# SSD scan of a hybrid layer: token columns and decay rows made once, the first tile in the last projection step, tiled matmul groups adjacent

## The chip, the cores and the metric

The kernel runs on one core of one Trainium2 chip. The metric is the device time of one execution in microseconds (us). Five engines work beside each other on the core: TensorE (PE; its weight loads have rows of their own, PEld), VectorE (DVE), ScalarE (ACT), GpSimd (POOL) and SyncE (SP), which only issues transfers.

## The reference

One layer of a streaming encoder for 1024 prompt tokens and 64 new tokens of another sequence (1088 tokens, width 1024, f32): FFN1, a token mixer of three head groups (SSD, GLA, forgetting attention), FFN2. The change concerns the SSD scan, 8 heads of 64, 2 groups of B and C, state 128. Cut to that:

```python
acum = jnp.cumsum(dt * A, axis=2)                       # within a chunk
cb = jnp.einsum('bclgn,bcsgn->bclsg', Cm, Bm)[..., hg]
seg = acum[:, :, :, None, :] - acum[:, :, None, :, :]
decay = jnp.where(causal, jnp.exp(jnp.where(causal, seg, 0.0)), 0.0)
y_intra = jnp.einsum('bclsh,bcsh,bcshp->bclhp', cb * decay, dt, x)
decay_end = jnp.exp(acum[:, :, -1:, :] - acum)
states = jnp.einsum('bclh,bclhn,bclhp->bchpn', decay_end * dt, Bh, x)
h = h * exp(acum[:, -1]) + states                        # scan over chunks, h0 first
y_inter = jnp.einsum('bclhn,bchpn,bclh->bclhp', Ch, h_prev, jnp.exp(acum))
y = y_intra + y_inter + ssd_d * xs                       # then * silu(z), norm, w_out
```

The prompt starts from a zero state, the 64 new tokens from a given one.

## The kernel before

All work lies on one core, and the order of every engine is written out by hand, with semaphores between engines. The layer runs FFN1, then 13 projection steps (`IN_PLAN`, t = 0 to 12, `proj_pe`, matmuls in the helper `three`, L169), then the SSD stage, the output projection (`out_pe`) and FFN2. Each projection step has up to two column blocks of three pieces of some 363 tokens; ACT reads each piece out of PSUM (L1328 copies, L1332 the Silu of the gates). Between the steps stand the small stages: the attention before t = 4, the GLA gate before t = 5, the GLA scan before t = 7 (`gla_pe`, `gla_act`, `gla_dve`), the convolution of x, B and C beside t = 7 to 10 (`conv_pool`, `conv_act`). t = 11 and 12 make the gates z. Small rows needed by the SSD scan (dt in `small`, the cumulated dt*A in `adt`) come out of step 2; `ssd_prep_dve` makes the cumulated sums by a scan. Eight of these rows, one for each head, hold all 1088 tokens. POOL sends `adt` to `a_kept` in HBM, and SP loads it back as a broadcast over 128 partitions, tile by tile, into `ab` (L2852, 512 KB each).

The SSD stage has nine tiles j, eight of 128 tokens and one of 64, the chunks of the scan. Its order on PE (`ssd_pe`): front(j) transposes B (L2066), the two small rows (L2067 and L2068, 8x128 each) and x (L2070) to token-major; cb(j) makes the scores of C and B (L2078); back(j) makes y and the state: H·cea, eight heads as 64-column matmuls (L2105), D times x (L2111), the tile's state (L2116), then x·dt times the masked scores, again eight heads in 64 columns (L2123). L2089 makes the sums for the norm of y, for two tiles at once. In the loop front(j+1) comes before back(j) and cb(j+1) after it.

ACT (`ssd_act`) makes exp of the decay rows of every tile (`ea`, L2165), copies B out of PSUM (L2171), two small exps (L2172, L2174), eight relus of a_s − a_l (L2180) and their exp (L2184); then squares, Ln and Exp for the norm, and casts of the mixed tiles for the output projection (L2191). The projection's Silu and these Exp are in different activation tables (loads at L1907, L2143 and at the first Silu). DVE (`ssd_dve`) copies the small columns (L2255, L2258), multiplies x by dt (`xdt`, L2285) and by dt times the decay to the end (`xde`, L2289), masks the scores (L2295), multiplies them into the decay (L2299), and updates the state: ht = H times the tile's decay (L2266), H = ht + state (L2271), and z = z times y (L2276). The decay in L2266 is read out of PSUM. POOL (`ssd_pool`) makes `dx` (D on the diagonal, L2334), `cea` = C times `ea` (L2320, two ops for a tile), the norm's multiplication (L2330) and the low parts of the mixed tiles (L2345). Behind the loop ACT and DVE split z for the output projection (`ssd_hi`, `ssd_lo`, L2224).

In the GLA stage ACT loads a table (L1907) and copies the outputs (L1910); DVE masks scores (L1988), takes the state out of PSUM (L1997) and updates S, with S and the new state in SBUF (L2012); PE's L1850 reads S. POOL has nothing to do there.

Of the kernel before, what the change touches and what calls it, by code (L numbers as in the profile page):

```python
# [2047 lines left out]

def ssd_pe(K, e, M):
    nc = K.nc  # L2050
    g = slice(SMALL_DT, SMALL_DT + SSD_H)
# [1 line left out]
    e.wait_ge(M.acum, 1)
    e.wait_ge(M.xc, 16)
    e.wait_ge(M.H, 1)

    def front(j):

        a, r = TILES[j]
        bank = 2 + j % 2  # L2060
        wait(e, M.b_read, j - 1)
        wait(e, M.sm_read, j - 1)
        wait(e, M.x_read, j - 1)
        wait(e, M.hupd, j - 1)
        for u in range(2):
            nc.tensor.transpose(K.ps[:r, bank, P * u:P * u + P], K.xc[:, 4 + u, a:a + r], K.ident)  # L2066
        nc.tensor.transpose(K.ps[:r, bank, 256:264], K.adt[g, a:a + r], K.ident[g, g])  # L2067
        nc.tensor.transpose(K.ps[:r, bank, 264:272], K.small[g, a:a + r], K.ident[g, g]).then_inc(M.b_mm, 1)  # L2068
        for u in range(4):
            mm = nc.tensor.transpose(K.ps[:r, j % 2, P * u:P * u + P], K.xc[:, u, a:a + r], K.ident)  # L2070
        mm.then_inc(M.x_mm, 1)

    def cb(j):

        a, r = TILES[j]
        wait(e, M.m, j)
        for u in range(2):
            mm = nc.tensor.matmul(K.ps[:r, 4, P * u:P * u + r], K.xc[:, 4 + u, a:a + r],  # L2078
                                  K.xc[:, 6 + u, a:a + r], start=True, stop=True)
        mm.then_inc(M.cb2_mm, 1)  # L2080
# [1120 lines left out]
```

## Time and profile before

| what | value |
|---|---|
| median of three runs | 2030.64 us (2027.94 to 2032.79) |
| the profiled execution, its own time | 2030.71 us |
| its span in the profile | 2028.9 us |
| granted TensorE clock | 0.998 |
| PE busy | 1990.9 us, 98% of the span |
| last projection matmul ends | 1158.67 us |
| SSD stage, to the first matmul of the output projection | 1158.67 to 1218.03 us |

The span is the time between the first and the last instruction that the profiler records; the execution's time has some 1.8 us around it. Times of rows are us from the span's start. An engine's idle time costs something only where PE waits for it. The start of a weight load (PEld) is a good mark for when a matmul group begins, as PE's own ends are modelled.

### The profile page before, as it was taken

To read this page: it belongs to the slowest core of one execution; us is meant where nothing else is said; L and a number is where in the kernel's file an instruction comes from. 1 tells how busy PE (TensorE), PEld (TensorE's weight loads), DVE (VectorE), ACT (ScalarE), POOL (GpSimd) and SP (SyncE) were. 2 spreads that over 40 slices of the span, in tenths; PEclk is the share of its full clock that TensorE was granted. 3 is DMA by queue.
4 is the path that set the end of the run, shared out by engine and by line. 5 is a ranking of instruction groups with operands and counts; after the bars stand their busy time and mean duration, and the time that the engine had idled before them with its cause. 6 is when DMAs were issued, how large, how long until landed. Compare 5 with 4: busy or idle time off the path is not lost.

```text
span 2028.9 us, 36007 instructions
## 1 busy us (share of the span) xinstructions
PE 1990.9 (98%) x15223; PEld 1935.0 (95%) x15223; DVE 1196.0 (59%) x1658; ACT 780.6 (38%) x1268; POOL 235.6 (12%) x295
## 2 busy tenths in 40 slices
PE   7999999999999999999999999999999999999999
PEld 7899999999999989768899989999999999999999
DVE  5955655556776752555555183377555565577674
ACT  6433333334333352664242393244333333343331
POOL 0000000000000340251011072100000000000000
PEclk9999999999999999999999999999999999999999
DMA  4222232225976514211011123312322223378654
GB/s 153 81 86 102 86 126 85 86 102 189 364 282 230 199 50 183 99 34 43 23 44 43 53 84 140 123 55 86 125 85 87 102 92 123 116 304 329 254 217 160
DMA packets 67330, 265.04 MB, mean 131 GB/s; under 512 B 7709, under 2 KB 20621, under 8 KB 57825
## 3 DMA queue, kind: packets, MB, share of 16 engines
q1 hardware_dynamic: 51648, 198.89, 27.2%
q0 software_dynamic: 15520, 63.83, 8.1%
q8 instruction: 121, 1.98, 0.4%
q14 instruction: 41, 0.33, 0.1%
HBM read 203.52 MB, written 59.18 MB: 129 GB/s over the span
## 4 chain that ended last, share of the span: by engine, by line
PE 90%; DVE 4%; DMA 3%; ACT 2%; issue 1%; POOL 0%; SPq 0%; DVEq 0%; ACTq 0%; POOLq 0%
PE ps L169 82%; PE ps L1485 1%; DMA h_kept<-sb_hs_b_last 1%; PE ps L1529 1%; PE ps L1511 1%; DMA sb_h_raw<-h_kept 1%; PE ps L247 1%; DVE sb_x L509 0%; DVE sb_xl L563 0%; PE ps L2123 0%; PE ps L2111 0%; PE ps L2089 0%; DVE sb_xl L499 0%; DMA sb_x<-x 0%; DMA sb_down_raw<-wb 0%
## 5 line engine op out<-in xcount | busy, mean ns | idle before, releaser
L169 PE MATMUL ps<-sb_xh,sb_up_hi 128*128 128x272 f32 x2400 | 692.0, 288 | 6.4 <-DVE sb_x L2448 2.0
L169 PE MATMUL ps<-sb_xl,sb_up_hi 128*128 128x272 f32 x2400 | 692.2, 288 | 0.0
L169 PE MATMUL ps<-sb_xh,sb_up_lo 128*128 128x272 f32 x2400 | 690.0, 287 | 0.0
L169 PEld LDWEIGHTS ps<-sb_xh,sb_up_hi 128*128 128x128 f32 x2400 | 452.9, 189 | 7.8 <-DVE sb_up_lo L454 2.3
L169 PEld LDWEIGHTS ps<-sb_xh,sb_up_lo 128*128 128x128 f32 x2400 | 452.4, 189 | 0.0
L169 PEld LDWEIGHTS ps<-sb_xl,sb_up_hi 128*128 128x128 f32 x2400 | 452.2, 188 | 0.1
L169 PE MATMUL ps<-sb_h_hi,sb_down_hi 128*128 128x272 f32 x1188 | 342.5, 288 | 0.6 <-DVE sb_down_lo L1049 0.4
L169 PE MATMUL ps<-sb_h_hi,sb_down_lo 128*128 128x272 f32 x1188 | 342.9, 289 | 0.0
L169 PE MATMUL ps<-sb_h_lo,sb_down_hi 128*128 128x272 f32 x1188 | 341.9, 288 | 0.0
L169 PE MATMUL ps<-sb_nh,sb_whi 128*128 128x362 f32 (+1 forms) x696 | 231.0, 332 | 2.4 <-DVE sb_nl L376 1.5
L169 PE MATMUL ps<-sb_nl,sb_whi 128*128 128x362 f32 (+1 forms) x696 | 228.3, 328 | 0.0
L169 PE MATMUL ps<-sb_nh,sb_wlo 128*128 128x362 f32 (+1 forms) x696 | 228.2, 328 | 0.0
L169 PEld LDWEIGHTS ps<-sb_h_hi,sb_down_hi 128*128 128x128 f32 x1188 | 223.5, 188 | 1.0 <-DVE sb_down_lo L1049 1.0
L169 PEld LDWEIGHTS ps<-sb_h_lo,sb_down_hi 128*128 128x128 f32 x1188 | 223.8, 188 | 0.0
L169 PEld LDWEIGHTS ps<-sb_h_hi,sb_down_lo 128*128 128x128 f32 x1188 | 223.4, 188 | 0.0
L447 ACT CAST sb_up_hi<-sb_up_sum 128x512 fp32r<-128x512 f32 x160 | 99.5, 622 | 241.2 <-PE ps L169 222.8
L454 DVE TENSOR_TENSOR sb_up_lo<-sb_up_raw,sb_up_hi 128x512 fp32r<-128x512 f32 x132 | 90.7, 691 | 132.9 <-ACT sb_up_hi L447 132.9
L1043 ACT CAST sb_down_hi<-sb_down_raw 128x1408 fp32r<-128x1408 f32 x54 | 74.2, 1374 | 225.2 <-PE ps L169 215.0
L169 PEld LDWEIGHTS ps<-sb_nh,sb_whi 128*128 128x128 f32 x696 | 130.7, 188 | 5.9 <-issue 2.3
L1162 DVE SCALAR_TENSOR_TENSOR sb_x<-ps,sb_x 128x544 f32<-128x544 f32 x96 | 65.4, 720 | 114.8 <-PE ps L169 114.8
L169 PEld LDWEIGHTS ps<-sb_nl,sb_whi 128*128 128x128 f32 x696 | 130.7, 188 | 0.6
L169 PEld LDWEIGHTS ps<-sb_nh,sb_wlo 128*128 128x128 f32 x696 | 130.7, 188 | 0.0
(340 smaller groups left out, 2729.1 us busy)
## 6 DMA issues: line engine op xcount, KB each, us to landing
sb_down_raw<-wb SPq DMA_DIRECT2D x92, 704.0 KB, 5.4
sb_up_raw<-wa SPq DMA_DIRECT2D x44, 1024.0 KB, 4.8
sb_h_raw<-h_kept SPq DMA_DIRECT2D x60, 544.0 KB, 6.0
sb_wraw<-wm SPq DMA_DIRECT2D x17, 1024.0 KB, 4.8
h_kept<-sb_hs_b POOLq DMA_DIRECT2D x20, 816.0 KB, 4.7
...
```

The source lines that it names most:

```text
L169: mm = K.nc.tensor.matmul(out, a, b, start=first and n == 0, stop=last and n == 2, skip_group_check=loose)
L247: mm = K.nc.tensor.matmul(K.ps[:, bank, :Q], K.ones, first_squares(K, c)[:, k], start=k == 0, stop=k == KT - 1)
L447: K.nc.scalar.copy(up_slot(K, n)[0], up_weight(K, n)).then_inc(N.f.ahi, 1)
L454: K.nc.vector.tensor_tensor(lo, up_weight(K, n), hi.bitcast(F32), ALU.subtract).then_inc(N.f.alo, 1)
L1043: K.nc.scalar.copy(down_slot(K, g)[0][:], down_raw(K, g, 0)).then_inc(N.f.bhi, 1)
L1162: K.nc.vector.scalar_tensor_tensor(out=x, in0=bank2(K, 2 * (g % 4)), scalar=0.5 * sign, in1=x, op0=ALU.mult, op1=ALU.add).then_inc(N.f.x_u ...
L1485: mm = nc.tensor.matmul(K.psf[:r, at:at + n], K.fq[o, m, a:a + r], rhs[o], start=True, stop=True)
L1511: mm = nc.tensor.transpose(K.ps[:w, 4 + n % 3, i * P:i * P + r], K.pr[u % PR][:r, k:k + w], K.ident[:r, :r])
L1529: mm = nc.tensor.matmul(K.ps[64 * s:64 * s + 64, 7, :r], v, K.pt[:w, s, i, :r], start=i == 0, stop=i == len(tiles) - 1)
```

## The change

1. **Token columns.** `ssd_tok_pe`, before projection step 8, transposes three rows of eight heads for all nine tiles (27 transposes of 8 rows): `adt`, dt, and dt times the decay to the end of the chunk. `ssd_tok_act` copies them to `tok` with two copies. The two small transposes, three small DVE operations and two small exps of each tile go.
2. **Decay rows.** `ssd_prep_dve` also makes a(end) − a (two subtractions). In the GLA stage ACT takes exp of both rows (8x1088 each) between the table load and the first copy; POOL sends exp(a) to `ea_kept` in HBM and multiplies the other by dt. SP loads `ea` of tiles 2 to 8 as a broadcast, as it does `ab`; tile 1's is still an exp on ACT. The state's decay, in L2266 before read out of PSUM, is now read from `ea` in SBUF.
3. **First tile.** After piece 3 of the last projection step PE does transposes and scores of tile 0 (banks 7, 6 and 4); ACT does its copy and relus after reading piece 2 and its exp after piece 3; DVE follows. Its operands have buffers of their own.
4. **Zero state.** Tile 0 has no H·cea matmuls and no `cea`; the first H is a copy of its state out of PSUM, and the memset goes.
5. **Order in back(j).** D times x, then the state, then H·cea and x·dt times scores, both in 64 columns, next to each other. The state's matmul thus comes before H·cea, and waits for xde and for the last H.
6. `dx` is made by POOL at the end of the convolution.

The core of the diff:

```diff
+        if t == IN_STEPS - 1 and n == IN_START[t] + FIRST_TILE_AT:
+            e.wait_ge(M.xc, 16)
+            ssd_front_pe(K, e, M, 0)
+            ssd_cb_pe(K, e, M, 0)
...
+    g = slice(SMALL_DT, SMALL_DT + SSD_H)
+    e.wait_ge(M.acum, 1)
+    nc.scalar.activation(K.ge[g, :], K.adt[g, :], ACT.Exp).then_inc(M.gexp, 1)
+    e.wait_ge(M.gqk, 1)
+    nc.scalar.activation(K.ga[g, :], K.go[g, 1], ACT.Exp).then_inc(M.gexp, 1)
+    e.wait_ge(M.gexp, 6)
...
+def ssd_rows_pool(K, e, M, ea_kept):
+    g = slice(SMALL_DT, SMALL_DT + SSD_H)
+    e.wait_ge(M.gexp, 5)
+    e.dma_start(ea_kept, K.ge[g, :]).then_inc(M.a_out, 16)
+    e.wait_ge(M.gexp, 6)
+    K.nc.gpsimd.tensor_tensor(K.ga[g, :], K.ga[g, :], K.small[g, :], ALU.mult).then_inc(M.pad, 1)
...
+def ssd_tok_pe(K, e, M):
+
+    g = slice(SMALL_DT, SMALL_DT + SSD_H)
+    e.wait_ge(M.st_read, GCH)
+    e.wait_ge(M.pad, 2)
+    for j, (a, r) in enumerate(TILES):
+        for q, rows in enumerate((K.adt, K.small, K.ga)):
+            at = 3 * SSD_H * j + SSD_H * q
+            mm = K.nc.tensor.transpose(K.ps[:r, 7, at:at + SSD_H], rows[g, a:a + r], K.ident[g, g])
+    mm.then_inc(M.b_mm, 1)
+
+
...
     def back(j):
 
         a, r = TILES[j]
+        xdt, xde, btok, seg = ssd_operands(K, j)
         wait(e, M.y2, j)
-        wait(e, M.hst_read, j)
-        if j == NTT - 1:
-            e.wait_ge(M.H, 2)
         y = K.ps[:, 5].rearrange("p (t q) -> p t q", t=4)
-        for h in range(SSD_H):
-            o = 64 * (h % 2)
-            if h % 4 == 0:
-                e.wait_ge(M.cea, 2 * j + h // 4 + 1)
-            mm = nc.tensor.matmul(y[o:o + 64, h // 2, :r], K.H[:, 64 * h:64 * h + 64], K.cea[:, j % 2, h, :r],
-                             start=h < 2, stop=False, skip_group_check=True)
-        mm.then_inc(M.h_read, 1)
         if j == 0:
             e.wait_ge(M.dx, 1)
         for u in range(4):
-            nc.tensor.matmul(y[:, u, :r], K.dx[:, u], K.xc[:, u, a:a + r], start=False, stop=False,
+            nc.tensor.matmul(y[:, u, :r], K.dx[:, u], K.xc[:, u, a:a + r], start=u == 0, stop=False,
                              skip_group_check=True)
-        e.wait_ge(M.b_read, j + 1)
+        e.wait_ge(M.b_read, j + 2)
         e.wait_ge(M.x_read, j + 1)
+        wait(e, M.hst_read, j)
         for u in range(2):
-            mm = nc.tensor.matmul(K.ps[:, 6, 256 * u:256 * u + 256], K.btok[j % 2][:r, P * u:P * u + P],
-                                  K.xde[:r, 256 * u:256 * u + 256], start=True, stop=True)
+            mm = nc.tensor.matmul(K.ps[:, 6, 256 * u:256 * u + 256], btok[:r, P * u:P * u + P],
+                                  xde[:r, 256 * u:256 * u + 256], start=True, stop=True)
         mm.then_inc(M.hst_mm, 1)
+        if j == NTT - 1:
+            e.wait_ge(M.H, 1)
+        if j:
+            for h in range(SSD_H):
+                o = 64 * (h % 2)
+                if h % 4 == 0:
+                    e.wait_ge(M.cea, 2 * (j - 1) + h // 4 + 1)
+                mm = nc.tensor.matmul(y[o:o + 64, h // 2, :r], K.H[:, 64 * h:64 * h + 64], K.cea[:, j % 2, h, :r],
+                                      start=False, stop=False, skip_group_check=True)
+            mm.then_inc(M.h_read, 1)
         e.wait_ge(M.m, j + 1)
         e.wait_ge(M.xdt, j + 1)
         for h in range(SSD_H):
             o = 64 * (h % 2)
-            mm = nc.tensor.matmul(y[o:o + 64, h // 2, :r], K.xdt[:r, 64 * h:64 * h + 64], K.seg[:r, j % 2, h, :r],
+            mm = nc.tensor.matmul(y[o:o + 64, h // 2, :r], xdt[:r, 64 * h:64 * h + 64], seg[:r, h, :r],
                                   start=False, stop=h >= 6, skip_group_check=True)
         mm.then_inc(M.y_mm, 1)
 
...
+    ssd_front_pe(K, e, M, 1)
+    ssd_cb_pe(K, e, M, 1)
     for j in range(NTT):
-        if j + 1 < NTT:
-            front(j + 1)
+        if 0 < j < NTT - 1:
+            ssd_front_pe(K, e, M, j + 1)
         back(j)
-        if j + 1 < NTT:
...
+def ssd_tok_act(K, e, M):
+
+    def copy():
+        e.wait_ge(M.out, 16 * (3 + 2 * GLA_H))
+        e.wait_ge(M.b_mm, 1)
+        tiles = K.ps[:, 7, :NTT * 3 * SSD_H].rearrange("p (j n) -> p j n", j=NTT)
+        K.nc.scalar.copy(K.tok[:, :NTT - 1], tiles[:, :NTT - 1])
+        K.nc.scalar.copy(K.tok[:TS, NTT - 1], tiles[:TS, NTT - 1]).then_inc(M.b_read, 1)
+
+    return {-1: copy}
+
...
+def ssd_first_act(K, e, M):
+
+    def tokens():
+        ssd_btok_act(K, e, M, 0)
+        ssd_seg_act(K, e, M, 0)
+
+    return {FIRST_TILE_AT - 1: tokens, FIRST_TILE_AT: lambda: ssd_exp_act(K, e, M, 0)}
 
...
+    M.dve(V.tensor_tensor_scan(K.adt[g, :], K.go[g, 1], K.go[g, 0], 0.0, ALU.mult, ALU.add))
+    for a, b, n in ((0, TP, P), (TP, T, TS)):
+        rows = K.adt[g, a:b].rearrange("p (c l) -> p c l", l=n)
+        to_end = V.tensor_tensor(K.go[g, 1, a:b].rearrange("p (c l) -> p c l", l=n),
+                                 rows[:, :, n - 1:n].to_broadcast([SSD_H, (b - a) // n, n]), rows, ALU.subtract)
+    to_end.then_inc(M.acum, 1)
...
+    def state(j):
+
         a, r = TILES[j]
...
+        if j == 0:
+            e.wait_ge(M.hst_mm, 1)
+            V.tensor_copy(K.H[:], K.ps[:, 6]).then_inc(M.hst_read, 1)
+        else:
+            e.wait_ge(M.h_read, j)
+            dst = K.Hp if j == TP // P - 1 else K.H
+            V.tensor_tensor(K.ht[:].rearrange("p (h q) -> p h q", h=SSD_H), hv,
+                            K.ea[:, j % 2, :, r - 1:r].to_broadcast([P, SSD_H, SSD_P]), ALU.mult).then_inc(M.hupd, 1)
+            e.wait_ge(M.hupd, j)
+            e.wait_ge(M.hst_mm, j + 1)
+            V.tensor_tensor(dst[:], K.ht[:], K.ps[:, 6], ALU.add).then_inc(M.hst_read, 1)
         if j == TP // P - 1:
             e.wait_ge(M.cache, 16 * (5 + GLA_H))
...
+        px = K.ps[:r, tile_banks(j)[0]].rearrange("p (h q) -> p h q", h=SSD_H)
+        for dst, at, done in ((xdt, SSD_H, M.xdt), (xde, 2 * SSD_H, M.x_read)):
+            V.tensor_tensor(heads(dst, r), px, K.tok[:r, j, at:at + SSD_H].rearrange("p (h o) -> p h o", o=1)
+                            .to_broadcast([r, SSD_H, SSD_P]), ALU.mult).then_inc(done, 1)
...
+    tokens(0)
+    decayed(0)
+    tokens(1)
+    state(0)
+    decayed(1)
+    for j in range(2, NTT):
+        state(j - 1)
+        tokens(j)
+        decayed(j)
...
+        if j == 1:
+            e.wait_ge(M.ea, 1)
+        else:
+            e.wait_ge(M.ea_in[j % 2], 16 * ((j - j % 2) // 2))
+        wait(e, M.h_read, j - 2)
...
+                    sp.wait_ge(M.a_out, 32)
                     sp.wait_ge(K.w_lo, 2 * s)
                     for j, (a, r) in enumerate(TILES):
-                        if j > 1:
-                            sp.wait_ge(M.ea, j - 1)
-                            sp.wait_ge(M.seg, j - 1)
+                        wait(sp, M.seg, j - 1)
+                        if j == 3:
+                            sp.wait_ge(M.ea, 1)
                         sp.dma_start(K.ab[:, j % 2, :, :r], o["a_kept"][:, a:a + r].partition_broadcast(P))\
                             .then_inc(M.a_in[j % 2], 16)
-                    sp.wait_ge(M.ea, NTT)
+                        if j < 2:
+                            continue
+                        if j == 2:
+                            sp.wait_ge(M.proj_mm, IN_START[IN_STEPS])
+                        else:
+                            sp.wait_ge(M.cea, 2 * (j - 2))
+                            sp.wait_ge(M.hupd, j - 2)
+                        sp.dma_start(K.ea[:, j % 2, :, :r], o["ea_kept"][:, a:a + r].partition_broadcast(P))\
+                            .then_inc(M.ea_in[j % 2], 16)
```

`ssd_front_pe` and `ssd_cb_pe` are front(j) and cb(j) as functions, without the small transposes.

## Rows read from the trace of the kernel before

**Rows 1.** the page, part 1: engine, busy us, share of the span, instructions.

```profile
PE 1990.9 (98%) x15223; PEld 1935.0 (95%) x15223; DVE 1196.0 (59%) x1658; ACT 780.6 (38%) x1268; POOL 235.6 (12%) x295
```

**Rows 2.** chain of waits, window 1157 to 1225: start us, us, engine, tile, line.

```profile
1159.18 1.28 ACT L2143
...
1160.48 1.06 ACT sb_ea L2165
...
1161.98 2.37 ACT sb_seg L2180 x8
...
1165.54 1.30 DVE sb_seg L2299 x2
```

**Rows 3.** windows: us; busy of PE, PEld, DVE, ACT, POOL; granted clock; DMA share; GB/s.

```profile
1166.88:1172.54 5.66, 5.66 (x56) 4.58 (x56) 5.52 (x12) 5.45 (x16) 3.00 (x3) 1.00 0.42 125
...
1183.88:1191.28 7.40, 7.40 (x66) 6.06 (x65) 5.40 (x12) 7.34 (x17) 4.98 (x3) 1.00 0.25 74
...
1209.92:1215.80 5.88, 5.88 (x57) 4.80 (x56) 5.27 (x11) 4.84 (x13) 2.59 (x3) 1.00 0.48 163
```

**Rows 4.** timeline of PE's weight loads, one tile: start, us, line, operands.

```profile
1173.57 0.52 PEld L2078 LDWEIGHTS ps<-sb_xc 128*128 128x128 f32 x4 [0.17 <-issue]
1174.01 0.25 PEld L2066 LDWEIGHTS ps<-sb_const,sb_xc 128*128 128x128 f32 x2
1174.43 0.13 PEld L2067 LDWEIGHTS ps<-sb_const,sb_cum 8*128 8x128 f32 x1 [0.17 <-issue]
1174.48 0.14 PEld L2068 LDWEIGHTS ps<-sb_const,sb_small 8*128 8x128 f32 x1
1174.64 0.42 PEld L2070 LDWEIGHTS ps<-sb_const,sb_xc 128*128 128x128 f32 x4
...
1176.26 0.97 PEld L2111 LDWEIGHTS ps<-sb_xc,sb_dx 128*128 128x128 f32 x8 [0.17 <-issue]
1177.14 0.73 PEld L2116 LDWEIGHTS ps<-sb_xde,sb_btok 128*128 128x128 f32 x4
1178.21 0.85 PEld L2123 LDWEIGHTS ps<-sb_seg,sb_xdt 128*64 128x64 f32 x16 [0.33 <-issue]
```

**Rows 5.** timeline of ACT, the last gate piece; in brackets the idle time before.

```profile
1158.69 0.47 ACT L1332 ACTIVATE sb_z<-ps 128x362 f32<-128x362 f32 x1 [3.53 <-PE ps L169]
```

**Rows 6.** timeline of DVE, the same tile.

```profile
1173.69 0.69 DVE L2276 TENSOR_TENSOR sb_z<-sb_z,ps 128x512 f32<-128x512 f32 x1 [0.28 <-PE ps L2123]
1174.29 0.68 DVE L2285 TENSOR_TENSOR sb_xdt<-ps,sb_tk 128x512 f32<-128x512 f32 x1
```

**Rows 7.** timeline of POOL in the SSD stage.

```profile
1177.91 2.51 POOL L2320 TENSOR_TENSOR sb_cea<-sb_xc,sb_ea 128x512 f32<-128x512 f32 x2 [3.33 <-ACT sb_ea L2165]
1180.38 2.52 POOL L2345 TENSOR_TENSOR sb_nl<-sb_fq,sb_nh 128x1088 fp32r<-128x1088 f32 x1
...
1219.97 2.37 POOL L2330 TENSOR_TENSOR sb_z<-sb_z,sb_scratch 128x1024 f32<-128x1024 f32 x1 [2.43 <-ACT sb_scratch L2159]
```

**Rows 8.** the tile ht: ns min/median/max, first and last start.

```profile
L2266 DVE TENSOR_TENSOR sb_ht<-sb_H,ps x9: 673/680/683, 1166.7 to 1214.6; 128x512 f32<-128x512 f32 x9
```

**Rows 9.** DMA of line L2852 (decay rows): us from issue to landing.

```profile
DMA to landing us min/median/max: 3.8/3.8/5.7
```

**Rows 10.** timeline of DVE behind the SSD loop.

```profile
1217.31 2.12 DVE L2224 SCALAR_TENSOR_TENSOR sb_nl<-sb_z,sb_vec,sb_nh 128x364 fp32r<-128x364 f32 x4 [0.31 <-ACT sb_nh L2215]
1220.71 2.02 DVE L2224 SCALAR_TENSOR_TENSOR sb_nl<-sb_z,sb_vec,sb_nh 128x362 fp32r<-128x362 f32 x1 [1.28 <-ACT sb_nh L2215]
```

**Rows 11.** line L1104 (FFN), ns min/median/max.

```profile
L1104 DVE TENSOR_TENSOR sb_h_lo<-sb_h_raw,sb_h_hi x72: 717/1285/2059, 514.0 to 1987.3; 128x1088 fp32r<-128x1088 f32 x60, 128x544 fp32r<-128x544 f32 x12
```

**Rows 12.** line L194 (norms), ns min/median/max.

```profile
L194 POOL TENSOR_TENSOR sb_rms<-sb_rms,sb_sqs x36: 817/972/2210, 680.2 to 1313.8; 128x362 f32<-128x362 f32 x24, 128x364 f32<-128x364 f32 x12
```

**Rows 13.** timeline of ACT in the GLA stage.

```profile
992.41 0.37 ACT L1910 COPY sb_go<-ps 128x256 f32<-128x256 f32 x1 [2.67 <-PE ps L1856]
```

**Rows 14.** timeline of DVE in the GLA stage.

```profile
992.25 0.48 DVE L2012 SCALAR_TENSOR_TENSOR sb_S<-sb_S,sb_glast,sb_gd 128x256 f32<-128x256 f32 x1
```

More of the change, by code:

```diff
@@ new lines, in ssd_front_pe @@
+def ssd_front_pe(K, e, M, j):
+    a, r = TILES[j]
+    x_bank, b_bank = tile_banks(j)
+    if j == 0:
+        e.wait_ge(M.b_read, 1)
+    elif j > 1:
+        e.wait_ge(M.b_read, j)
+        e.wait_ge(M.x_read, j - 1)
+    for u in range(2):
+        mm = K.nc.tensor.transpose(K.ps[:r, b_bank, P * u:P * u + P], K.xc[:, 4 + u, a:a + r], K.ident)
+    mm.then_inc(M.b_mm, 1)
+    for u in range(4):
+        mm = K.nc.tensor.transpose(K.ps[:r, x_bank, P * u:P * u + P], K.xc[:, u, a:a + r], K.ident)
+    mm.then_inc(M.x_mm, 1)
@@ L2049, in ssd_pe, with ssd_cb_pe, ssd_operands @@
+def ssd_cb_pe(K, e, M, j):
+    a, r = TILES[j]
+    wait(e, M.m, j)
+    for u in range(2):
+        mm = K.nc.tensor.matmul(K.ps[:r, 4, P * u:P * u + r], K.xc[:, 4 + u, a:a + r],
+                                K.xc[:, 6 + u, a:a + r], start=True, stop=True)
+    mm.then_inc(M.cb2_mm, 1)
+def ssd_operands(K, j):
+    if j == 0:
+        return K.xdt_first, K.xde_first, K.btok_first, K.seg_first
+    return K.xdt, K.xde, K.btok[j % 2], K.seg[:, j % 2]
 def ssd_pe(K, e, M):
     nc = K.nc
-    g = slice(SMALL_DT, SMALL_DT + SSD_H)
@@ L2052, in ssd_pe @@
     e.wait_ge(M.proj_read, IN_START[IN_STEPS])
[L2053 to L2080, printed above, removed]
     def sums(c):
@@ L2138, in ssd_pe, with ssd_btok_act, ssd_seg_act, ssd_exp_act @@
     return lambda: sums(NYP - 1)
+def ssd_tok_act(K, e, M):
+    def copy():
+        e.wait_ge(M.out, 16 * (3 + 2 * GLA_H))
+        e.wait_ge(M.b_mm, 1)
+        tiles = K.ps[:, 7, :NTT * 3 * SSD_H].rearrange("p (j n) -> p j n", j=NTT)
+        K.nc.scalar.copy(K.tok[:, :NTT - 1], tiles[:, :NTT - 1])
+        K.nc.scalar.copy(K.tok[:TS, NTT - 1], tiles[:TS, NTT - 1]).then_inc(M.b_read, 1)
+    return {-1: copy}
+def ssd_btok_act(K, e, M, j):
+    r = TILES[j][1]
+    e.wait_ge(M.b_mm, j + 2)
+    wait(e, M.hst_mm, j - 1)
+    K.nc.scalar.copy(ssd_operands(K, j)[2][:r, :], K.ps[:r, tile_banks(j)[1], 0:256]).then_inc(M.b_read, 1)
+def ssd_seg_act(K, e, M, j):
+    r = TILES[j][1]
+    seg = ssd_operands(K, j)[3]
+    e.wait_ge(M.a_in[j % 2], 16 * (j // 2 + 1))
+    wait(e, M.y_mm, j - 1)
+    for h in range(SSD_H):
+        ins = K.nc.scalar.activation(seg[:r, h, :r], K.ab[:r, j % 2, h, :r], ACT.Relu,
+                                     bias=K.tok[:r, j, h:h + 1], scale=-1.0)
+    ins.then_inc(M.seg, 1)
+def ssd_exp_act(K, e, M, j):
+    r = TILES[j][1]
+    seg = ssd_operands(K, j)[3]
+    e.wait_ge(M.seg, j + 1)
+    K.nc.scalar.activation(seg[:r, :, :r], seg[:r, :, :r], ACT.Exp, scale=-1.0).then_inc(M.eseg, 1)
+def ssd_first_act(K, e, M):
[3 more added lines that the diff above has]
+    return {FIRST_TILE_AT - 1: tokens, FIRST_TILE_AT: lambda: ssd_exp_act(K, e, M, 0)}
 def ssd_act(K, e, M):
@@ L2302, in operands, with ssd_dx_pool @@
         ins.then_inc(M.m, 1)
-    decays(0)
-    for j in range(NTT):
-        if j:
-            state(j - 1)
-        operands(j)
-    state(NTT - 1)
+    tokens(0)
[7 more added lines that the diff above has]
+        decayed(j)
+    state(NTT - 1)
+def ssd_dx_pool(K, e, M):
+    e.wait_ge(M.b_mm, 1)
+    e.wait_ge(M.a_out, 32)
+    for u in range(4):
+        ins = K.nc.gpsimd.tensor_scalar(K.dx[:, u], K.ident, K.vec[:, V_D + u:V_D + u + 1], 1.0, ALU.mult, ALU.mult)
+    ins.then_inc(M.dx, 1)
 def ssd_pool(K, e, M, outs):
@@ L2658, in __init__ @@
         self.ea = sem(tag + "ea")
-        self.de0 = sem(tag + "de0")
-        self.de1 = sem(tag + "de1")
-        self.sm_read = sem(tag + "sm_read")
+        self.ea_in = [sem(tag + f"ea_in{s}") for s in range(2)]
         self.cea = sem(tag + "cea")
```

121 lines of the change are left out of this document (46 added, 75 removed).

## The prediction

> **What bounds the kernel now.** First the page: TensorE (PE) is busy 98% of the span [rows 1]. So time is won only where PE waits or where PE's own work shrinks, and work on another engine is free until PE waits for it. Then the chain of waits through the SSD stage: after the last projection matmul at 1158.67 the chain leaves PE for ACT (table load 1.28, exp of the decay rows 1.06, eight relus 2.37, one more exp) and DVE (1.30), and PE has it back at 1166.88 [rows 2]. The table of windows, cut where the matmul group L2123 of each tile starts, shows the rest: PE is busy for the whole of every window after 1166.88, with DVE at 5.5 and ACT at 5.4 of 5.66 [rows 3]. A tile takes 5.66, one with the norm's sums 7.40. So the stage has two prices: a start of 8.2 in which PE waits for ACT and DVE, and a loop in which PE is the bound and the others are close behind. Last, PE's weight loads show the parts of one tile and the gaps between them [rows 4]. The granted clock is 1.00 (2.4 GHz) in all windows [rows 3], so no clock effect enters.
>
> E is the end of the last projection matmul, 1158.67; numbers without a unit are us.
>
> **The change part by part.**
>
> *Start (gain).* Before, L2123 of tile 1 starts at 1172.54 [rows 3], E+13.87. After, tile 0's transposes, scores and mask lie in the last projection step, so PE starts when the last gate piece is read: .02+.47+.06 = .55 [rows 5]. Then by the rows of one tile [rows 4]: transposes of tile 1 .66 (L2066 .25, L2070 .42, without the small pair), scores .44 (L2078 to L2066), tile 0's D-skip .88 (L2111 to L2116), state and gap 1.07 (L2116 to L2123), its group .85: E+4.44. Then PE to DVE .30 (idle .28 before L2276) and z .69 [rows 6], in which the transposes of tile 2 fit: D-skip of tile 1 from E+5.5, state and gap, and now H·cea .85 before the group: L2123's successor in tile 1 starts at E+8.3. The other engines are just in time [rows 2]: table load done E+1.79, exp 1.06, copy (.44 with the two small ops that go), relu 2.37, exp 1.06 at E+6.7, DVE 1.30: E+8.1. POOL's cea(1), 2.51 [rows 7] behind the first exp, is there at E+5.4. Gain 13.87 − 8.3 = **5.6**.
>
> *Loop (gain).* From tile 1 to tile 8 L2123 goes from 1172.54 to 1215.80, 43.3 [rows 3]. PE's work of a tile after: .66+.44+.88+1.07, two groups of .85, one gap of .17 = 4.91 [rows 4], against 5.66. But PE will not be the bound. The new order closes a ring: z → xdt → xde (.60+.60+.69, by the spacing of DVE's rows) → state and gap 1.07 → H·cea .85 → .30 → ht .68 → H .69 → z: 5.5 [rows 4, 6, 8]. Four steps of 5.5 and three with sums, which PE bounds (4.91 + 1.74 (7.40 − 5.66) − .17 for a gap = 6.5), make 41.5; the shorter last tile gives back .4: 41.1. Gain **2.1**. ACT loses its row exp and is no bound. SP's queue now holds two broadcasts a tile, and a load is queued behind a wait for cea and ht; one lands in 3.8, at worst 5.7 [rows 9], and ea(j) is wanted about a tile (5.5) after its issue; what is late there, 0 to .2, lies under the next term.
>
> *ht reads SBUF twice (loss).* Before, every large DVE op of the loop has one input in PSUM, and ht is .67 to .68 in all nine tiles though POOL works beside it [rows 8]. After, ht multiplies H by ea, both in SBUF. What such an op does beside POOL shows at L2224: .53 each in a row of four, but 2.02 when asked at 1220.71 [rows 10], while POOL's norm runs 1219.97 to 1222.34 [rows 7]: it ended .39 after the norm, so it got going about .2 before the norm's end. L1104, two SBUF inputs too, grows from 1.29 to 2.06 [rows 11], and POOL's L194 from .97 to 2.21 [rows 12]: each of the two loses in turn. After the change cea(j+2) starts behind H·cea and its load, some 3.95 after ht, and ht is asked again 4.8 after, inside the first half of cea (1.25) [rows 7]. So a wait of .2 to .8 a tile, and none in the tiles with sums, where PE is later anyway. I take **1.0** in all; bounds .3 (POOL elsewhere) and 2.5 (most tiles).
>
> The Trainium skill ("SBUF — State Buffer", Who interferes with whom) says that a VectorE instruction with two SBUF inputs contends with a GpSimd instruction that reads SBUF, and that the one that issues second blocks for the whole instruction. The trace agrees: 2.02 against .53 [rows 10].
>
> *Token columns (loss).* 27 transposes of 8 rows at step 8 stand on PE's path, in the projection, where PE is full. Two such loads follow each other at .05, though one lasts .14 [rows 4]. 27 × .055 = 1.5, with two gaps of .17 **1.9**; bounds 1.5 and, at .14 each and the gaps, 4.2. The two ACT copies lie beside pieces of 4.0, of which ACT is idle 3.53 [rows 5].
>
> *First tile in the last step (loss).* Transposes .66 and scores .44 now stand before E: **1.1**, with two gaps 1.45 [rows 4]. ACT has 3.53 idle in a piece [rows 5]; between pieces 3 and 4 it does read .47, load 1.28, exp 1.06, load 1.28: 4.1, .1 late against a PE that runs up to three pieces ahead. Nothing; without that cover 2.6 for the two loads.
>
> *GLA stage (loss).* Two exps of 8x1088 go where ACT is idle 2.67 before its first copy [rows 13]; by the 1.06 of a 1024 exp [rows 2] they take 2.2 and fit. Then POOL sends ea_kept and multiplies 8x1088 out of SBUF; 128x1088 take 2.52 [rows 7], and I give 8 rows the same. It starts near 992.0. DVE's L2012, two SBUF inputs, asks at 992.25 in a stretch without idle, and PE waits for its S in each chunk [rows 14]. By the hand-over above: 992.0 + 2.5 − .2 − 992.25 = **2.1**; bounds 0 (if 8 rows are short) and 2.5. The two DVE subtractions added to step 3's preparation meet no wait of PE.
>
> *Rest.* The D matrices (four 128x128 ops, some .35 each by elements against cea's 1.25 for 512) move to POOL's idle stretch; without that cover they stand ahead of cea(1), which has 2 in hand. The sums behind the loop wait a little more, as ssd_hi(0) now needs tile 8's H chain whole: **.4**, bounds .3 and .9.
>
> Sum: 5.6+2.1−1.0−1.9−1.1−2.1−.4 = 1.2 gained: 2030.71 − 1.2 = **2029.5**. The profiled execution's own time is 2030.71 (span 2028.9 and 1.8 around it), .07 above the median of 2030.64, so nothing is to be corrected.
>
> **The rivals.**
> - *Faster: the port costs nothing.* If ht and L2012 don't meet POOL (the 8-row op is short, cea starts behind ht) and the transposes take 1.5: 5.6+2.1−1.5−1.1−.4 = 4.7, 2026.0. For: the waits hang on tenths of a us in POOL's start. Against: L2224 met POOL in the same neighbourhood [rows 10], and DVE in the GLA stage is full.
> - *Slower: ht loses the port for POOL's whole queue.* Mechanism: a waiting ht gets the port when POOL pauses, not between two POOL ops in line, and POOL has such lines (cea, cea, nl 2.52, norm 2.37) [rows 7]. A wait is then up to 2.5, and the loop ends about 4.4 later: 2033.9; with transposes at .14 each 2036. It makes the kernel slower than before once the eight waits come to .15 a tile (1.2/8) more than taken, and by 0.2% at .65 more. Against: L194 and L1104 lose in turn [rows 11, 12].
> - *It doesn't do what it says: adjacency gains nothing.* PE's saving of .75 a tile goes to idle, as the ring (5.5) exceeds 4.91. My sum has this already; were the ring 5.7 (.1 more at two of its hand-overs) the loop would gain .8 less: 2030.3.
>
> **How the numbers follow.** About 0.2% (4.1) is what a measurement of this kernel tells from no change. Forecast and third rival: .60. Port free: .24, with the few tenths beyond 4.1 that it needs. Port held for the queue, or several terms at their worse ends: .16. Best ends (5.6+2.1−.3−1.5−1.1−0−.3 = 4.5) give 2026.2, worst ends (7.7−2.5−4.2−1.45−2.5−.9 = −3.9) 2034.6. The range leaves about a tenth on each side: 2025.8 to 2033.6.
>
> **What would show it.** E some 5 later than before (1.9+1.1+2.1) and the group of tile 1 at E+8.3; PE idle in the loop, released by DVE's H or xde; tiles of 5.5 to 5.8. ht longer than .68 where POOL runs; one L2012 of about 2.5 near 992 beside an 8x1088 op on POOL; two table loads in the last projection step without idle of PE. Wrong would be: no long ht and no long L2012 (first rival), ht of 2 or more in most tiles (second), or transposes over 3.

## The result and the profile after

The changed kernel takes 2036.74 us, the median of six runs (2035.84 to 2038.80), against 2029.27 for the kernel before (six runs): a ratio of 1.0034, 95% interval 1.002 to 1.0047. It is slower by 7.5 us, outside the range of 2025.8 to 2033.6. Its profiled execution has a span of 2036.7 against 2028.9, 7.8 more. The whole of it, and more, comes from a place where the prediction had put 2.1: TensorE's clock falls to its lower level, 1.2 GHz, in the GLA stage.

Part 2 of the page shows it: the granted clock in 40 slices of the span, before and after.

```profile
PEclk9999999999999999999999999999999999999999
```

```profile
PEclk9999999999999999999799999999999999999999
```

The 7 is the slice from 967 to 1018. The windows table of that stretch gives the clock (the column behind POOL's; the others as in [rows 3]):

```profile
987.00:990.00 3.00, 2.64 (x24) 1.69 (x22) 2.66 (x6) 2.99 (x3) 0.52 (x1) 0.97 0.02 5
990.00:993.00 3.00, 3.00 (x19) 1.74 (x18) 2.95 (x3) 0.52 (x2) 2.47 (x1) 0.50 0.08 12
...
1008.00:1011.00 3.00, 3.00 (x28) 2.37 (x24) 2.26 (x5) 0.01 (x1) 0.00 (x0) 0.50 0.00 0
...
1023.00:1026.00 3.00, 3.00 (x17) 3.00 (x16) 0.00 (x0) 0.18 (x1) 0.70 (x1) 0.84 0.13 10
```

The clock reads 1.00 up to 987, .97 in the next window and .50 from 990 on; it is back only at 1023.9, in the projection that follows. Before it fell, PE was busy 2.64 of 3.00, with pauses; afterwards PE reads busy nearly all the time, but at half the clock. Such pauses are not new. In the kernel before, the same part of the stage has PE busy 1.59 and 1.72 of 2.00, and the clock holds:

```profile
988.00:990.00 2.00, 1.59 (x21) 0.91 (x14) 1.47 (x3) 1.72 (x3) 0.00 (x0) 1.00 0.04 8
990.00:992.00 2.00, 1.72 (x18) 1.23 (x18) 1.90 (x5) 0.00 (x0) 0.00 (x0) 1.00 0.00 0
```

In the same stretch DVE's state update (L2012 before, L2027 now, [rows 14]) and POOL's new multiplication meet as foretold:

```profile
990.54 2.45 DVE L2027 SCALAR_TENSOR_TENSOR sb_S<-sb_S,sb_glast,sb_gd 128x256 f32<-128x256 f32 x1
```

```profile
990.23 2.47 POOL L2047 TENSOR_TENSOR sb_ga<-sb_ga,sb_small 8x1088 f32<-8x1088 f32 x1 [0.27 <-ACT sb_ga L1921]
```

The update asked at 990.54, .3 behind POOL's op of 2.47, takes 2.45 in place of .48.

The rest of the change shows in five more views. The weight loads of PE in the SSD stage (last group of tile 1, last group of tile 8; compare [rows 3, 4]):

```profile
1180.81 0.91 PEld L2170 LDWEIGHTS ps<-sb_seg,sb_xdt 128*64 128x64 f32 x16
...
1225.06 0.54 PEld L2170 LDWEIGHTS ps<-sb_seg,sb_xdt 64*64 64x64 f32 x16
```

The chain of waits there, with the last projection read, the three ht that wait, and the first matmuls of the output projection:

```profile
1172.62 0.48 ACT sb_z L1336
...
1186.62 1.71 DVE sb_ht L2341
...
1205.28 2.94 DVE sb_ht L2341
...
1218.48 1.49 DVE sb_ht L2341
...
1227.66 2.00 PE ps L169 x12
```

POOL's operations that these ht meet (asked at 1186.62, 1205.28 and 1218.48):

```profile
1186.48 2.97 POOL L2416 TENSOR_TENSOR sb_cea<-sb_xc,sb_ea 128x512 f32<-128x512 f32 x2 [5.96 <-DMA sb_ea<-ea_kept]
...
1205.15 2.51 POOL L2437 TENSOR_TENSOR sb_nl<-sb_gg,sb_nh 128x1088 fp32r<-128x1088 f32 x1
...
1217.04 2.37 POOL L2426 TENSOR_TENSOR sb_z<-sb_z,sb_scratch 128x1024 f32<-128x1024 f32 x1
```

The 27 token transposes, the first of them between two loads of the projection:

```profile
1049.22 0.19 PEld L169 LDWEIGHTS ps<-sb_nh,sb_wlo 128*128 128x128 f32 x1
1049.64 0.13 PEld L2085 LDWEIGHTS ps<-sb_const,sb_cum 8*128 8x128 f32 x1 [0.23 <-issue]
...
1051.32 0.19 PEld L169 LDWEIGHTS ps<-sb_nh,sb_whi 128*128 128x128 f32 x1
```

And ACT in the last projection step, where the two extra table loads and the first tile's exp stand between two reads (compare [rows 5]):

```profile
1165.13 1.28 ACT L2225 ACT_TABLE_LOAD   x1
...
1167.50 1.28 ACT L1336 ACT_TABLE_LOAD   x1
1168.80 0.47 ACT L1336 ACTIVATE sb_z<-ps 128x362 f32<-128x362 f32 x1
```

For the sum, three marks are taken from the chain of waits: the gate read that opens the GLA stage, the projection matmuls behind it, and the first matmuls of the output projection. Before:

```profile
986.00 0.48 ACT sb_gg L1332
...
1010.92 4.16 PE ps L169 x24
...
1218.41 2.00 PE ps L169 x12
```

The last mark is the first matmul, .38 behind its weight load at 1218.03.

After (the last mark, 1227.66, stands above):

```profile
984.28 0.48 ACT sb_gg L1336
...
1020.13 5.94 PE ps L169 x24
```

With these rows the difference of the two traces adds up. E (the end of the last projection matmul) is at 1172.60 now, 13.93 later.

| stretch | before | after | difference |
|---|---|---|---|
| up to the gate read that opens the GLA stage | 986.00 | 984.28 | −1.72 |
| from there to the next projection matmul | 24.92 | 35.85 | +10.93 |
| from there to E | 147.75 | 152.47 | +4.72 |
| E to the first matmuls of the output projection | 59.74 | 55.06 | −4.68 |
| the rest | 810.49 | 809.04 | −1.45 |
| span | 2028.9 | 2036.7 | +7.80 |

The first and the last line are not of the change: the trace of the kernel before with one added POOL operation (e2 below) opens the stage at 983.86 and has 808.66 behind the SSD stage. They belong to the one execution that was profiled before, which is 1.4 above the median of six. Of the +4.72, 1.8 is the end of the low clock (the first 24 projection matmuls take 5.94 in place of 4.16). The block is what the long update lasts beyond the usual .48, 2.45 − .48 = 2.0. So the low clock costs 10.93 − 2.0 + 1.8 = 10.7. The trace of e5 below gives the price a second time, as there the clock falls without any block.

In the GLA stage the clock can also fall without that POOL operation (e5 below). The table in the next section therefore counts, beside each median, the runs whose mean granted clock is .993 or less. The five profiled executions with a fall there have .991 to .993, the others .997 to 1.000. In a run that was not profiled the mean shows that the clock fell, not where.

### The profile page after: what moved, and what is told of

Its sections match the earlier page's. It is cut to its first block, busy times and chain, and to the rows that moved or that the text cites. A ratio compares the mean times of both kernels' runs of the same rounds, so it can differ in the third digit from the quotient of the medians.

```text
span 2036.7 us, 35919 instructions
## 1 busy us (share of the span) xinstructions
PE 1997.7 (98%) x15216; PEld 1944.0 (95%) x15216; DVE 1199.2 (59%) x1631; ACT 776.8 (38%) x1248; POOL 238.5 (12%) x295
## 3 DMA queue, kind: packets, MB, share of 16 engines
q8 instruction: 120, 1.97, 0.4%
## 4 chain that ended last, share of the span: by engine, by line
PE 92%; DVE 4%; ACT 2%; issue 1%; DMA 1%; POOL 0%; SPq 0%; DVEq 0%; ACTq 0%
PE ps L169 84%; PE ps L1494 1%; PE ps L1538 1%; PE ps L1520 1%; PE ps L247 1%; PE ps L2147 0%; DVE sb_x L509 0%; PE ps L2153 0%; DVE sb_xl L563 0%; DMA sb_x<-x 0%; PE ps L1846 0%; DVE sb_xl L499 0%; PE ps L1865 0%; PE ps L2163 0%; DVE sb_x L548 0%
```

## The experiments

Two causes were open. First, the clock: in the trace of the change it fell at 989.80 (.99 from 989.75 to there, .50 behind it), when POOL's multiplication had not begun; so the fall could be due to the block, or come by itself. Second, the SSD stage: ht waits in the trace, but is it these waits that hold the loop at 44.25 (1180.81 to 1225.06), where 41.1 + 1.0 was forecast?

| kernel | median us (runs) | ratio to before, 95% | runs at .993 or less |
|---|---|---|---|
| before, in the three sessions | 2028.98 (24), 2028.73 (30), 2030.22 (19) | | 0 of 24, 0 of 30, 5 of 19 |
| the change | 2036.74 (6) | 1.0034 [1.002, 1.0047] | 6 of 6 |
| the change again | 2037.78 (10) | 1.0019 [0.9999, 1.0039] | 9 of 10 |
| e1: multiplication at the end of GLA | 2027.64 (10) | 0.9996 [0.9979, 1.0012] | 2 of 10 |
| e2: before, with the multiplication | 2039.54 (4) | 1.0043 [1.0026, 1.006] | 4 of 4 |
| e3: decay in PSUM | 2036.62 (9) | 1.0035 [1.0025, 1.0046] | 9 of 9 |
| e4: e1 and e3 | 2026.35 (10) | 0.9989 [0.9973, 1.0005] | 2 of 10 |
| e4 again | 2023.57 (10) | 0.9979 [0.996, 0.9997] | 2 of 10 |
| e5: e4 in the old order | 2024.73 (10) | 0.9989 [0.9971, 1.0006] | 3 of 10 |
| e6: before, with POOL only writing | 2030.24 (10) | 1.0002 [0.9992, 1.0013] | 1 of 10 |
| e7: e4, first tile behind E | 2033.48 (10) | 1.0024 [1.0012, 1.0036] | 1 of 10 |
| e8: the change, multiplication in four | 2027.79 (10) | 0.9997 [0.9972, 1.0022] | 2 of 10 |

The first two sessions (e1 to e7) ran on one chip, the third (e8 and the change again) on another.

**e1, the multiplication moved.**

```diff
 def ssd_rows_pool(K, e, M, ea_kept):
...
-    e.wait_ge(M.gexp, 6)
-    K.nc.gpsimd.tensor_tensor(K.ga[g, :], K.ga[g, :], K.small[g, :], ALU.mult).then_inc(M.pad, 1)
 def gla_pool(K, e, M, outs):
+    g = slice(SMALL_DT, SMALL_DT + SSD_H)
     e.wait_ge(M.S_end, 1)
+    e.wait_ge(M.gexp, 6)
+    K.nc.gpsimd.tensor_tensor(K.ga[g, :], K.ga[g, :], K.small[g, :], ALU.mult).then_inc(M.pad, 1)
```

> The changed kernel, with POOL's 8x1088 multiplication moved from the middle of the GLA stage to its end. Theory S (the stall): POOL's op takes the port from DVE's state update, PE runs dry, and TensorE's clock falls to 1.2 GHz for the rest of the stage; without it the update is back at .48, the granted clock stays 1.00 there, and the kernel is 2.0 + 8.9 + 1.8 = some 12 us faster than the change, near 2024.5. Theory P (phase): the clock falls for a reason of its own (in the trace of the change it fell at 989.85, .4 before POOL's op began at 990.23); then only the 2.0 us of the block go, near 2034.7, and the clock still reads .50 in the stage.

Measured: 2027.64, and 2024.8 to 2025.9 in four of its ten runs. In the chain of waits the stage runs from the gate read to the first projection matmul in 24.92, to the hundredth what it took before:

```profile
984.02 0.48 ACT sb_gg L1336
...
1008.94 4.21 PE ps L169 x24
```

No state update is longer than .49 and the clock is 1.00. Theory S comes near in size: 12 were expected, and the medians are 9.1 apart. But two of ten runs still have a mean clock of .990 and .991 and take 2036.6 and 2038.0. If they fell in this stage, the fall does not need the block; the trace of e5 shows one that did not.

**e2, the multiplication alone, in the kernel before.**

```diff
+            e.wait_ge(M.att, 2)
+            nc.gpsimd.tensor_tensor(K.ga[dt, :], K.ga[dt, :], K.small[dt, :], ALU.mult).then_inc(M.pad, 1)
             gla_pool(K, e, M, o)
```

> The kernel before, with the same POOL multiplication of 8x1088 (into rows that nothing reads afterwards) at the same place of the GLA stage, and nothing else of the change. Theory S: one state update of some 2.5 us, the clock at 1.2 GHz for the rest of the stage, 12 us slower than before: near 2041. Theory P: 2.0 us slower, near 2031.3, and the clock stays at 2.4 GHz.

Measured: 2039.54, 10.6 over before where 12 was expected, all four runs at .991 or .992. One POOL instruction of 2.48 on eight partitions costs more than the whole change loses. Here the order of events is plain: DVE's update, PE's wait for it, and the windows (columns as in [rows 3]).

```profile
990.11 2.51 DVE L2013 SCALAR_TENSOR_TENSOR sb_S<-sb_S,sb_glast,sb_gd 128x256 f32<-128x256 f32 x1
```

```profile
993.13 0.48 PE L1838 MATMUL ps<-sb_gv,sb_kt 64*128 64x256 f32 x1 [1.86 <-DVE sb_gd L1998]
```

```profile
990.00:993.00 3.00, 1.27 (x14) 0.61 (x10) 2.93 (x3) 0.37 (x1) 2.34 (x1) 1.00 0.00 0
993.00:995.00 2.00, 1.87 (x18) 1.67 (x18) 1.90 (x5) 0.00 (x0) 0.00 (x0) 0.76 0.00 0
995.00:1015.00 20.00, 20.00 (x156) 15.42 (x153) 14.54 (x30) 2.23 (x6) 0.00 (x0) 0.50 0.00 1
```

PE has nothing for 1.86, is busy 1.27 of 3.00, and .9 after it goes on the clock falls: .76 in that window, then .50 for twenty us. It is back at 1021.4, 2.4 into the projection, though PE reads busy for the whole of the twenty us. The trace of the change run again shows the same order, with a pause of 1.79 before the fall, and so does that of e3 (1.80):

> The changed kernel itself beside it: 2036 to 2039 in every run, with the clock at .991 to .993 in the mean.

```profile
990.00:995.00 5.00, 3.21 (x35) 2.37 (x36) 4.86 (x7) 0.80 (x2) 2.71 (x2) 1.00 0.05 7
995.00:1010.00 15.00, 15.00 (x118) 11.61 (x116) 11.31 (x24) 1.49 (x4) 0.00 (x0) 0.50 0.00 1
```

9 of its 10 runs, and all 6 of the first measurement, have the low clock; the tenth took 2031.18 at .995. With e2 and e3 that makes 28 of 29 runs with the whole multiplication at that place. Where it is elsewhere, or cut (e1, e4 twice, e5, e8), the change has 11 of 50. So the block makes nearly certain what otherwise happens now and then, and the profiled execution of the change happened to be one in which the clock fell a moment before the block. Without the block the change still has falls on the first chip, 9 of 40, where the kernel before has none in 54; what else in it makes them likelier was not tried.

The Trainium skill ("TensorE: Matmul & The Clock Gate", Part 1: The HAM clock gate) says that the gate judges PE's activity in windows that run free of the kernel's start, so that the moment of a transition shifts from run to run. The counts in the table fit that, as the same instruction stream keeps the clock in eight runs and loses it in two; the windows themselves no run here shows.

**e6, POOL at work there, but only writing.** Three memsets of 8x1088 in place of the multiplication:

```diff
+            for p in (0, 64):
+                nc.gpsimd.memset(K.ga[p:p + SSD_H, :], 0.0)
+            nc.gpsimd.memset(K.ga[dt, :], 0.0).then_inc(M.pad, 1)
```

> The kernel before with POOL at work at the same place of the GLA stage, but only writing: three memsets of 8x1088 in place of the multiplication of the earlier run. Theory (the port): a POOL op that reads nothing from SBUF takes nothing from DVE's state update, the update stays at .48, PE sees nothing, the clock stays at 2.4 GHz and the time is that of before, 2029 within 2. Rival (POOL's work at that place by itself, or its writes, are what costs): the update is long again and the time is near 2039.5, as with the multiplication.

Measured: 2030.24, ratio 1.0002. POOL's three memsets run from 990.18 to 993.25 (the first two shown), and all fifteen updates of DVE take .485:

```profile
990.18 2.03 POOL L3064 MEMSET sb_ga<- 8x1088 f32 x2 [28.71 <-DVE sb_attn L1989]
```

```profile
L2013 DVE SCALAR_TENSOR_TENSOR sb_S<-sb_S,sb_glast,sb_gd x15: 485/485/485, 987.9 to 1005.9; 128x256 f32<-128x256 f32 x15
```

So it is not that POOL works there, nor that it writes. What the memsets lack is the reading of SBUF while DVE wants two inputs from there. The Trainium skill ("SBUF — State Buffer", Who interferes with whom) says just that: such a VectorE instruction contends with a GpSimd instruction that reads SBUF, not with one that only writes it; .485 here and 2.51 in e2 agree.

**e8, the multiplication cut into four, at its place in the change.**

```diff
-    K.nc.gpsimd.tensor_tensor(K.ga[g, :], K.ga[g, :], K.small[g, :], ALU.mult).then_inc(M.pad, 1)
+    for a in range(0, T, T // 4):
+        ins = K.nc.gpsimd.tensor_tensor(K.ga[g, a:a + T // 4], K.ga[g, a:a + T // 4], K.small[g, a:a + T // 4], ALU.mult)
+    ins.then_inc(M.pad, 1)
```

> The changed kernel with POOL's 8x1088 multiplication cut into four of 8x272 at the same place, nothing else. By 2.47 for 1088 columns each takes some .65. Theory (hand-over between ops): DVE's state update gets the port after the op that is running, so an update waits .5 at most, and POOL's next op waits for DVE in its turn; the block on PE falls from 2.0 to 1 or less, spread over two or three updates. Then if the clock falls because of one long pause, it now holds in most runs: 2036.7 - 10.7 - 1 = 2025. Rival (DVE gets the port only when POOL's queue is empty): an update of some 2.5 again, the clock at 1.2 GHz in every run, 2036 to 2038.

Measured: 2027.79; eight of ten runs keep the clock. DVE and POOL:

```profile
990.09 0.74 DVE L2027 SCALAR_TENSOR_TENSOR sb_S<-sb_S,sb_glast,sb_gd 128x256 f32<-128x256 f32 x1
```

```profile
989.78 3.36 POOL L2048 TENSOR_TENSOR sb_ga<-sb_ga,sb_small 8x272 f32<-8x272 f32 x4 [0.27 <-ACT sb_ga L1921]
...
990.51 0.93 POOL L2048 TENSOR_TENSOR sb_ga<-sb_ga,sb_small 8x272 f32<-8x272 f32 x1
```

The first line of POOL is all four ops, the second the second of them alone. One update waits .26 and one .04 (.52 at 992.91), and POOL's four ops take 3.36 in all where one took 2.47. The update asked at 990.09 is done at 990.83, while the second POOL op, next in line at 990.51, takes .93 where the first took .76: DVE gets its turn between two POOL ops that stand in line. The stage takes 25.21 (983.84 to 1009.05), .3 over e1. The same arithmetic, at the same place, on the same engine, is 10 us cheaper in the median when it is cut (2027.79 against 2037.78 in the same session).

**e3 and e4, the decay read out of PSUM.** ACT writes the tile's eight decays beside B's transpose, as before the change, and ht reads them there; front(j) waits for ht two tiles back.

```diff
+        nc.scalar.activation(K.ps[:, 2 + j % 2, 296:304], K.ab[:, j % 2, :, TILES[j][1] - 1], ACT.Exp)\
+            .then_inc(M.dec, 1)
...
-                            K.ea[:, j % 2, :, r - 1:r].to_broadcast([P, SSD_H, SSD_P]), ALU.mult).then_inc(M.hupd, 1)
+                            K.ps[:, 2 + j % 2, 296:304].rearrange("p (h o) -> p h o", o=1)
+                            .to_broadcast([P, SSD_H, SSD_P]), ALU.mult).then_inc(M.hupd, 1)
```

> The changed kernel with the tile's decay read out of PSUM again, as before the change (a small exp on ACT writes it), so that ht has one input in SBUF. The GLA stage is left as in the change. Theory: the long ht rows (1.69, 2.93, 1.48) are waits for POOL's port; all ht rows fall to .68, and the loop from tile 1 to tile 8 falls from 44.25 to 41.5 to 42: the kernel is 2 to 3 us faster than the change, near 2034. Rival: the ring of the new order is held by something else (loads of ea, cea on POOL), and then the loop stays within .5 of 44.2.

> Both edits at once: POOL's multiplication at the end of the GLA stage and the decay in PSUM. Under theory S and the port theory the two gains add: 12 + 2.5 below the change, near 2022, that is 7 us (0.35%) faster than before. Under theory P near 2032.

> The kernel with both repairs once more, beside the others: 2023.3 to 2025.5 where the clock holds (five of ten earlier), 10 more where the clock falls.

Measured: e3 2036.62 in the total, beside 2036.74 and 2037.78 for the change in two other sessions, too close to call; all its nine runs have the low clock of the GLA stage, where nothing was altered. In the trace the SSD stage did what the theory says. All ht (the tile's row in e3), and the last groups of tiles 1 and 8 in e4:

```profile
L2347 DVE TENSOR_TENSOR sb_ht<-sb_H,ps x8: 686/687/689, 1182.1 to 1223.0; 128x512 f32<-128x512 f32 x8
```

```profile
1167.97 0.91 PEld L2172 LDWEIGHTS ps<-sb_seg,sb_xdt 128*64 128x64 f32 x16
...
1209.00 0.54 PEld L2172 LDWEIGHTS ps<-sb_seg,sb_xdt 64*64 64x64 f32 x16
```

The loop takes 41.03 in e4 (1209.00 − 1167.97), and 3.2 more in the change. E to the output projection is 51.85 in e4 (1159.76 to 1211.61), against 55.06 in the change and 59.74 before. Both repairs together, e4, are the best version: 2026.35 and 2023.57 in two sessions, faster than before in the second (0.9979, interval below 1), inside its interval of no change in the first. For e4 2022 was expected; five of ten runs lie between 2023.3 and 2025.5 in the first session, and eight of ten between 2021.9 and 2024.2 in the second. On the total time alone e3 would have been called without effect; its trace has E to the output projection in 51.85, as e4.

**e5, the old order in back(j), on top of e4.** H·cea, D-skip, state, then the scores' group, as in the kernel before.

```diff
+        wait(e, M.hst_read, j)
+        if j:
+            for h in range(SSD_H):
...
+            mm.then_inc(M.h_read, 1)
         for u in range(4):
...
         mm.then_inc(M.hst_mm, 1)
-        if j:
-            for h in range(SSD_H):
...
-            mm.then_inc(M.h_read, 1)
```

> The two repairs (POOL's multiplication at the end of the GLA stage, decay in PSUM) with the order of the kernel before in back(j): H·cea, D times x, state, x·dt times scores; the 64-column groups are apart again. Theory (the ring bounds the new order): in the trace with both repairs a tile takes 5.49 though PE's work is 4.9; with the old order the state's chain is shorter, PE is the bound at 4.9 + two mode gaps of .17 = 5.28 a tile, and the loop from tile 1 to tile 8 falls from 41.0 to about 40.6: adjacency gains nothing. Rival (adjacency is worth its gaps): each tile is .34 longer, the loop 43.4.

Measured: 2024.73. Loads of the last groups of tiles 1 and 8:

```profile
1173.98 0.85 PEld L2172 LDWEIGHTS ps<-sb_seg,sb_xdt 128*64 128x64 f32 x16 [0.33 <-DVE sb_seg L2388]
...
1215.11 0.55 PEld L2172 LDWEIGHTS ps<-sb_seg,sb_xdt 64*64 64x64 f32 x16 [0.33 <-issue]
```

The loop is 41.13, against 41.03 in the new order; 40.6 was expected, and 43.4 by the rival of this run. Setting the tiled groups side by side gains .1, as the third rival of the prediction had it: what PE saves (two gaps) goes into the ring. A tile without sums is 5.3 in the old order and 5.5 in the new, one with sums 7.0 and 6.7. Its profiled execution is one of the three with a fallen clock, and there POOL's multiplication does not run beside the updates, of which none is longer than .49. Its windows, and the marks of its stage in the chain of waits:

```profile
986.00:988.00 2.00, 1.59 (x18) 0.91 (x14) 1.54 (x3) 1.97 (x4) 0.00 (x0) 1.00 0.04 8
988.00:990.00 2.00, 1.72 (x16) 1.26 (x16) 1.90 (x5) 1.79 (x2) 0.52 (x1) 0.87 0.00 0
...
1008.00:1010.00 2.00, 2.00 (x22) 1.33 (x20) 1.39 (x3) 0.37 (x1) 0.00 (x0) 0.51 0.00 0
1010.00:1012.00 2.00, 2.00 (x33) 1.65 (x30) 1.76 (x4) 0.29 (x1) 0.00 (x0) 1.00 0.00 0
```

```profile
983.93 0.48 ACT sb_gg L1336
...
1014.83 4.20 PE ps L169 x24
```

Three things follow. PE's shares before the fall, 1.59 and 1.72, are those of the kernel before, where the clock held: PE's busy share does not tell the two apart. The clock is back at 1009.95, inside the GLA stage and not in the projection, with PE reading 2.00 of 2.00 on both sides. And the fall alone has a price: 20.5 us at 1.2 GHz make the stage 30.90 long in place of 24.92, .29 for each us. At that rate the 30.3 us that the change spends in the stage at 1.2 GHz are 8.8; its stage lost 10.93 − 2.0 = 8.9 beside the block.

**e7, the first tile prepared behind the last step again,** otherwise e4.

```diff
-        if t == IN_STEPS - 1 and n == IN_START[t] + FIRST_TILE_AT:
-            e.wait_ge(M.xc, 16)
-            ssd_front_pe(K, e, M, 0)
-            ssd_cb_pe(K, e, M, 0)
...
+    ssd_front_pe(K, e, M, 0)
+    ssd_cb_pe(K, e, M, 0)
     ssd_front_pe(K, e, M, 1)
...
+    ssd_btok_act(K, e, M, 0)
+    ssd_seg_act(K, e, M, 0)
+    ssd_exp_act(K, e, M, 0)
```

> Both repairs, and the preparation of the first tile behind the last projection step again (transposes, scores, copy, relus, exp, mask). By the durations of the trace tile 0's masked scores are ready at E+7.0 (table load 1.28, copy .3, relus 2.4, exp 1.06, mask 1.3) and the last group of tile 1 starts at E+11.7 in place of 8.2, while E is 1.1 earlier: 2.4 slower than with both repairs. Rival (the preparation is hidden by something else late, such as the load of ea(2) or cea(1)): no difference beyond the 1.1.

Measured: 2033.48, 9.9 over e4 in the same session where 2.4 was expected. The windows of the start:

```profile
1162.00:1164.00 2.00, 0.00 (x0) 0.00 (x0) 0.00 (x0) 1.97 (x5) 0.00 (x0) 1.00 0.02 6
1164.00:1166.00 2.00, 0.45 (x2) 0.45 (x3) 1.78 (x3) 2.00 (x7) 0.86 (x1) 0.59 0.88 256
1166.00:1168.00 2.00, 2.00 (x11) 2.00 (x11) 0.70 (x2) 1.97 (x8) 1.65 (x2) 0.50 0.99 251
```

Tile 0's mask is ready at E+7.0 (1165.51), as worked out. But PE comes back at .50, and tile 1's last group starts at E+16.8 (1175.29), not 11.7. From E to 1165.55 PE is busy 1.98 of 7.04. The kernel before has as long a start and keeps the clock (1.00 from 1158.67 to 1166.88); there PE is busy 5.95 of 8.21, with two tiles' transposes and the matmuls of H·cea on the zero state, which the change leaves out. That this filling kept the clock is an argument from the two traces and was not tried by itself. In the change the preparation stands in the last step, and the pause is short: from E to tile 1's group PE is busy 7.66 of 8.21, and the clock reads 1.00.

## Why the prediction was wrong

- **The clock.** The step that failed is the sentence "so no clock effect enters". It was read from the windows of the SSD stage, where it is true, and then used for the whole change. The GLA stage was priced at the length of the block, 2.1; measured is 2.0 for the block, at the place that was foretold, and 10.7 for the clock behind it. The forecast shows no window of the GLA stage. There the trace before has 1.00 throughout, so the fall could not be read off it; but it also has PE busy 1.59 and 1.72 of 2.00, and the change takes PE's work away for two us more. None of the rivals had it.
- **ht's waits, a term of the sum mis-sized.** The mechanism is as told, also that DVE's turn comes between two POOL ops (e8). But 1.0 was reckoned with halves of cea (1.25) as the blocker, and waits of .2 to .8. The rows show whole operations there too: ht waits 1.0 behind a cea (1.69), .3 behind another (.94 at 1193.11), 2.2 behind an nl of 2.51 that had begun .13 earlier (2.93), and .8 behind norm (1.48). What the loop lost is 3.2 (44.25 − 41.03), past the bound of 2.5. With it the loop is 1.0 longer than before (44.25 against 43.26), not 1.1 shorter.
- **The start** was forecast at E+8.3 and is at E+8.2: 5.7 gained for 5.6. **The loop without waits**: 41.1 forecast, 41.03 measured in e4; the ring of 5.5 a tile is as worked out. In part the total is luck: the two whole tiles with sums take 6.7 in place of 6.5, and the short last one takes 5.74, .8 below 6.5 where .4 was reckoned.
- **Token transposes**: the projection's loads on both sides are 2.10 apart, .17 in the ordinary case: 1.9, as forecast. They follow each other at .06 (the forecast's own figures, 27 × .055 and two gaps, make 1.8). **First tile on PE's path**: 1159.00 to 1160.32, less .17: 1.15 for 1.1. **Table loads**: the read behind them came .2 late and PE did not wait, as forecast. **Tail**: forecast .4 late, measured 2.60 from the last group to the output projection against 2.61: nothing. **D matrices**: 3.67 for the four where some 1.4 was reckoned, in POOL's idle stretch as foretold, so PE waits for none.
- **The base.** The sum starts from 2030.71, the one execution that was profiled; the median of six is 2029.27, 1.4 lower. From there the gain of 1.2 leads to 2028.1.
- **The rivals.** "Faster, port free" failed at both places. "Slower, port held for POOL's queue" named nearly the right time for a wrong reason: e8 shows the hand-over. "Adjacency gains nothing" is right (e5).

Without the fall of the clock the measured terms are 5.66 − .99 − 1.93 − 1.15 − 1.97 = −.4: no change that a measurement of this kernel tells. For the work that was priced the forecast (1.2 faster) was right to 1.6, and the time was decided by what was not priced.
